# Attention: query units 6 to 8 projected whole in three steps, unit 9 in token halves

## The reference

```
proj = h @ w_in + b_in                        # (512, 1024) @ (1024, 1280)
q, k, v = split(proj, [1024, 1152])           # 16 query heads of 64, 2 key/value heads
q = q * 64 ** -0.5; k, v: previous and own block of 128 tokens
s = where(band, q @ k.T, -inf)                # band: the 128 latest keys
mx = max(max(s), sink)
p = exp(s - mx) / (sum(exp(s - mx)) + exp(sink - mx))
out = (p @ v) @ w_out + b_out
```

## Time and profile before

| | us |
|---|---|
| median of 3 runs | 1103.65 (1103.55 to 1104.68) |
| the profiled execution, its own time | 1103.78 |
| its span, first to last instruction | 1102.0 |
| TensorE busy | 1089.2 (99%) |
| VectorE busy | 532.7 (48%) |
| ScalarE busy | 430.8 (39%) |
| GpSimd busy | 51.5 (5%) |

### The profile page before, as it was taken

One profiled execution on the slowest core, in us unless ns is written; L12 is line 12 of the kernel. 1 busy time (PEld: TensorE's weight loads), 2 busy tenths in 40 slices (PEclk: granted clock), 3 DMA queues, 4 the chain that ended last, 5 costly groups with the idle time before them and its releaser, 6 DMA issues.

```text
span 1102.0 us, 14768 instructions
## 1 busy us (share of the span) xinstructions
PE 1089.2 (99%) x5562; PEld 911.0 (83%) x5562; DVE 532.7 (48%) x797; ACT 430.8 (39%) x750; POOL 51.5 (5%) x52
## 2 busy tenths in 40 slices
PE   9999998999999999999999999999999999999997
PEld 7888886898888888888889987789888888888886
DVE  7544567653434343333366586664444434523344
ACT  6511455543332323322255276754232323422242
POOL 1000210000000000000002023300000000000000
PEclk9999999999999999999999999999999999999999
DMA  8342327123233332122272632022323232303231
GB/s 267 112 116 80 112 95 212 38 78 114 84 107 92 98 99 92 39 95 95 95 191 59 162 87 77 1 67 87 114 77 114 76 114 78 112 26 101 99 136 77
DMA packets 141764, 109.51 MB, mean 99 GB/s; under 512 B 22480, under 2 KB 127088, under 8 KB 141728
## 3 DMA queue, kind: packets, MB, share of 16 engines
q1 hardware_dynamic: 140720, 105.84, 32.4%
q0 software_dynamic: 864, 2.92, 0.9%
q10 hardware_dynamic: 144, 0.26, 0.1%
HBM read 106.87 MB, written 2.13 MB: 99 GB/s over the span
## 4 chain that ended last, share of the span: by engine, by line
PE 92%; DVE 4%; ACT 3%; issue 0%; POOL 0%; DVEq 0%; ACTq 0%; POOLq 0%
PE ps L1461 17%; PE ps L1462 17%; PE ps L1463 17%; PE ps L1713 7%; PE ps L1711 7%; PE ps L1712 7%; PE ps L1656 3%; PE ps L1657 2%; PE ps L1658 2%; PE ps L1545 1%; PE ps L1547 1%; PE ps L1546 1%; PE ps L1801 1%; PE ps L1830 1%; PE ps L1812 1%; ACT w_hi L556 1%
## 5 line engine op out<-in xcount | busy, mean ns | idle before, releaser
L1461 PE MATMUL ps<-act_hi,w_hi 128*128 128x512 f32 (+1 forms) x1016 | 368.0, 362 | 0.1
L1463 PE MATMUL ps<-act_hi,w_lo 128*128 128x512 f32 (+1 forms) x1016 | 366.4, 361 | 0.0
L1462 PE MATMUL ps<-act_lo,w_hi 128*128 128x512 f32 (+1 forms) x1016 | 366.4, 361 | 0.0
L1461 PEld LDWEIGHTS ps<-act_hi,w_hi 128*128 128x128 f32 x1016 | 191.8, 189 | 30.8 <-DVE w_lo L916 0.9
L1463 PEld LDWEIGHTS ps<-act_hi,w_lo 128*128 128x128 f32 x1016 | 191.8, 189 | 29.3
L1462 PEld LDWEIGHTS ps<-act_lo,w_hi 128*128 128x128 f32 x1016 | 191.8, 189 | 28.7
L1711 PE MATMUL ps<-w_hi 128*128 128x512 f32 x288 | 112.0, 389 | 0.0
L1712 PE MATMUL ps<-w_lo,w_hi 128*128 128x512 f32 x288 | 112.0, 389 | 0.0
L1713 PE MATMUL ps<-w_hi,w_lo 128*128 128x512 f32 x288 | 112.0, 389 | 0.0
L749 ACT ACTIVATE arena<-ps,vecs 128x512 f32<-128x512 f32 x44 | 34.3, 780 | 188.6 <-PE ps L1463 188.6
L1242 DVE SCALAR_TENSOR_TENSOR arena<-ps,vecs,arena 128x511 f32<-128x511 f32 x44 | 33.0, 749 | 144.4 <-ACT arena L749 144.4
(11 more groups left out here) (210 smaller groups left out, 1220.1 us busy)
## 6 DMA issues: line engine op xcount, KB each, us to landing
raw<-in_f_w_up SPq DMA_DIRECT2D x88, 512.0 KB, 4.6
raw<-in_f_w_down SPq DMA_DIRECT2D x44, 512.0 KB, 3.3
raw<-in_m_w_in SPq DMA_DIRECT2D x23, 512.0 KB, 4.8
raw<-in_m_w_out SPq DMA_DIRECT2D x8, 512.0 KB, 3.4
raw<-in_a_w_in SPq DMA_DIRECT2D x16, 256.0 KB, 4.4
raw<-in_a_w_out SPq DMA_DIRECT2D x16, 256.0 KB, 4.8
h<-in_x SPq DMA_DIRECT2D x4, 512.0 KB, 7.4
h<-in_x_turned SPq DMA_DIRECT2D x3, 512.0 KB, 8.0
```

What stands on the lines that cost most here:

```text
L1461: nc.tensor.matmul(dst, uh[:, k], zh, start=(k == 0), stop=False)
L1462: nc.tensor.matmul(dst, uh[:, k], zl, start=False, stop=False)
L1463: ins = nc.tensor.matmul(dst, ul[:, k], zh, start=False, stop=(k == KT - 1))
```

## The change

Units 6, 7 and 8 are projected over all 512 tokens at once: unit 6 after scores(0), unit 7 in step 0, unit 8 in step 1. Unit 9 is projected in halves, at the head of steps 2 and 3, ahead of scores(s + 1). In step 2 turn_probs(2) now comes ahead of scores(3). VectorE adds the biases of units 6, 7 and 8 whole. That of unit 6 stands between the splits of units 8 and 9; those of 7 and 8 stand where the second halves stood in steps 0 and 1; the halves of unit 9 follow inverse(2) and inverse(3), ahead of masked_max. The counts that scores, the reuse of bank 5 and the first output part wait for are changed to match.

```diff
@@ add_a_bias (VectorE)
-                if n >= 6 and part == 0:
-                    dve.wait_ge(qb_mm, n - 5)
+                if n == A_UNITS - 1 and part == 0:
+                    dve.wait_ge(qb_mm, 1)
@@ VectorE, ahead of the steps
             masked_max(0)
-            for n in range(6, A_UNITS):
-                if n < 8:
-                    split_lo(G_AIN + n + 2)
-                add_a_bias(n, 0, 0, S // 2)
+            split_lo(G_AIN + 8)
+            add_a_bias(6)
+            split_lo(G_AIN + 9)
             dve.wait_ge(va_mm, 1)
@@ VectorE, step s
+                if s in (2, 3):
+                    add_a_bias(A_UNITS - 1, s - 2, (s - 2) * S // 2, (s - 1) * S // 2)
                 if s + 1 < AT_STEPS:
                     masked_max(s + 1)
                 if s >= 3 and s % 2 == 1:
                     mixed_lo((s - 3) // 2)
                 for k in OUT_SPLITS.get(s, []):
                     split_lo(G_AOUT + k)
-                if s < 4:
-                    add_a_bias(6 + s, 1, S // 2, S)
+                if s < 2:
+                    add_a_bias(7 + s)
@@ scores (TensorE)
-                pe.wait_ge(pj_used, QK_UNITS + (5 if s < 2 else A_UNITS if s < 6 else A_UNITS + 4))
+                pe.wait_ge(pj_used, QK_UNITS + (5 if s < 2 else 8 if s == 2 else A_UNITS + (s >= 2 * ASTEPS)))
@@ out (TensorE)
-                        pe.wait_ge(pj_used, QK_UNITS + A_UNITS + 4)
+                        pe.wait_ge(pj_used, QK_UNITS + A_UNITS + 1)
@@ TensorE
+            def query(n, lo=0, hi=S):
+
+                pe.wait_ge(w_lo_done, counted(G_AIN + n))
+                ins = project(SLOT[G_AIN + n], a_bank(n), lo, hi)
+                if hi == S:
+                    ins.then_inc(w_used, 1)
+                else:
+                    ins.then_inc(qb_mm, 1)
+
             scores(0)
-            for n in range(6, A_UNITS):
-                pe.wait_ge(w_lo_done, counted(G_AIN + n))
-                if n == 9:
-                    pe.wait_ge(pj_used, QK_UNITS + 7)
-                project(SLOT[G_AIN + n], a_bank(n), 0, S // 2).then_inc(qb_mm, 1)
+            query(6)
             turn_values()
...
             for s in range(AT_STEPS):
                 last = s + 1 == AT_STEPS
+                if s in (2, 3):
+                    pe.wait_ge(pj_used, QK_UNITS + (7 if s == 2 else A_UNITS))
+                    query(A_UNITS - 1, (s - 2) * S // 2, (s - 1) * S // 2)
+                if s == 2:
+                    turn_probs(s)
                 if not last:
                     scores(s + 1)
...
-                if s < 4:
-                    pe.wait_ge(pj_used, QK_UNITS + A_UNITS + s // 3)
-                    project(SLOT[G_AIN + 6 + s], a_bank(6 + s), S // 2, S).then_inc(w_used, 1)
-                turn_probs(s)
+                if s < 2:
+                    query(7 + s)
+                if s != 2:
+                    turn_probs(s)
```

## The result

The changed kernel takes 1108.69 us (median of 5 runs, 1107.62 to 1110.37) against 1104.61 for the kernel before; the ratio is 1.0041, 95% interval 1.0028 to 1.0054. It is slower, as forecast, but by 4.1 us at the median and not by 3.3, and 1108.69 lies above the range (1104.5 to 1108.3).

The account below looks back on a forecast made before the run. TensorE, busy 99% of the span, was taken to bound the kernel, so any wait there lengthens it. Terms -0.82 + 2.65 + 0.20 + 1.30 made +3.3 us, predicting 1107.0 us, range 1104.5 to 1108.3.

Parts of the forecast that it names:

- The clock falls: Rival: after the new idle stretch TensorE gets the lower clock for a unit, 5.5 us dearer, 1112.5 us; chance 0.04.
- Projection: TensorE's projection of units 6 to 9: fewer matmul starts take it from 23.52 to 22.70 us, a gain of 0.82.
- scores(2): TensorE idles 2.65 us (2.3 to 3.4) for unit 7's bias, queued on VectorE behind output weight 1's late load and split.
- Step 2: Ahead of scores(3), TensorE idles 0.20 us (0 to 0.4) for the bias of unit 9's first half.
- Steps 3 and 4: Softmax chain loses cover: idle 0.6 us ahead of scores(5), 0.7 ahead of step 4's transposes; together 1.3 (0.6 to 1.8).
- Step 3's own transposes: Block 0's softmax chain, 4.82 us plus 0.15, just covered by TensorE's 5.05 us of work; cost taken as 0.

Follow-up runs that it names:

- changed_again: The changed kernel, unaltered, measured once more on the same chip as the other runs: median 1107.88 us, ratio 1.0038 to the kernel before.
- half1_cut: Changed kernel with unit 9's second half cut in two, 12 matmuls ahead of scores(4), 12 behind mix(0), its bias moved: 1108.96 us, ratio 1.0039 to before.
- filled_transposes: Changed kernel with twenty unused 128x128 transposes in TensorE's idle stretch ahead of scores(2): median 1107.68 us, ratio 1.0032 to the kernel before.
- split9_first: Changed kernel with VectorE's split_lo of unit 9 put ahead of the bias of unit 6: median 1108.31 us, ratio 1.0039 to the kernel before.

## Why the prediction was wrong

The direction, the chain of waits and the sum of their terms were right; the step that failed is the rival "The clock falls". It had no term in the sum and no place in the range, and it came in the very execution that is the median: 1108.69 less its 1.57 us is 1107.12, and the forecast for the profiled execution was 1107.1. Term by term, from the timeline above:

- Projection: forecast -0.82. Queries 6 and 7 at 5.58 and 5.59 us, query 8 at 5.60 (in changed_again, without the fall) and two halves at 2.95 and 3.05 make 22.77 for 22.70: -0.75. The trace, with its 12 ns per start, was the right guide, and the 0.18 us estimated from the 2.5 ns of the Trainium skill ("TensorE: Matmul & The Clock Gate", section on 56 ns against 53.3 ns) would have been wrong.
- scores(2): forecast 2.65 (2.3 to 3.4). Measured 635.92 - 632.82 - 0.53 = 2.57, and in the same way 2.66 in changed_again and 3.17 in half1_cut. One small piece was read too short: a whole unit's bias begins 0.20 us after the block (626.26 behind 626.06), not 0.11.
- Step 2: forecast 0.20. The profile's wait is 0.23; by the starts it is 647.88 - 647.04 - 0.53 = 0.31, and the transposes of step 1 took 0.35 where I gave them 0.53: 0.13 together.
- Steps 3 and 4: forecast 0.6 + 0.7. Measured 654.79 - 653.65 - 0.53 = 0.61, and 659.38 - 655.86 - 2.90 = 0.62.
- Step 3's own transposes: forecast just covered; no wait shows there.
- The clock: "TensorE might be granted the lower clock for a unit", chance 0.04, price 5.5 us. The lower clock was granted for some 3.3 us and not for the whole unit, which costs 1.57 us, and it came in about five of the ten executions of this kernel (counted by time and mean clock). In the profiled one it makes +3.2 into +4.76, and it puts the median of the first set above the range. The size of this surplus is in part luck: the second set, with one such execution of five, has its median of 1107.88 inside the range.

Why I gave it 0.04: 1.7 us idle between 165 and 170 us at a clock of 1.00 was read as evidence that idle time does not matter. It was shorter than the wait that I forecast, and one execution. The trace of before has a second such case, which I had not read:

```profile
177.40 0.47 PE L1656 MATMUL ps<-w_hi,act_hi 128*128 128x512 f32 x1 [1.74 <-DVE w_lo L916]
```

All eleven profiled executions have both, 1.70 to 1.75 us each, at a granted clock of 1.00 from 165 to 185 us. So for 1.7 us the evidence is better than I knew, and for 2.2 to 3.1 us it does not hold: there two traces of four show the fall. The Trainium skill's rule ("TensorE: Matmul & The Clock Gate", "HAM oscillation") that gaps between bursts bring the clock down stood beside it, though the waits in that section's own case are longer than these. The changed kernel's windows agree with it (0.50 behind 2.51 us of idle time), changed_again's do not (1.00 behind 2.59). Had both been weighed, the case belonged inside the range with a chance near a half. That the same gap ends in a fall in one execution and not in another is shown; what decides it is open.

A second term was missing: the start. The first four matmuls of 512 columns, in the kernel before and in changed_again:

```profile
5.69 1.19 PE L1489 MATMUL ps<-act_hi,w_hi 128*128 128x512 f32 x4
```

```profile
5.71 2.01 PE L1490 MATMUL ps<-act_hi,w_hi 128*128 128x512 f32 x4
```

From their start to that of the next four it is 1.03 us in the one and 1.84 in the other, at a granted clock of 1.00 in both profiles. The rest of the kernel is later by it: scores(0) starts at 619.81, 619.84 and 620.58 in before, the changed kernel and changed_again. The profiled execution of before, from which I added up, was one without that delay. The delay is seen in kernels with and without the gap and is no effect of the change, but it widens what a range has to hold by up to 1 us. With it the profiled times add up: 1103.78, plus the change of the stretch, plus the lateness of scores(0), gives the time of each of the ten other profiled executions to 0.15 us (changed_again 1107.84 for 1107.83, the changed kernel 1108.57 for 1108.69). So the edits changed nothing outside the stretch.

The start and the fall go together in the few traces there are. Of the four with TensorE idle for over 2 us, the fall is in the two where scores(0) came early (619.84, 619.94), and not in the two where it came late (620.58, 620.80). An early start with the fall ends at 1108.7, a late one without it at 1107.8; the 1107.1 of the forecast needs an early start without the fall, and none of the ten executions is under 1107.62. filled_transposes, with an early start (620.01) and the gap filled, took 1107.53. Four traces can't show that the start decides on the fall, and nothing here tests it.

## What to carry to other kernels

A block moved on a saturated engine is cover for a chain elsewhere: before merging blocks to save starts (here some 10 ns each, 0.75 us in all), list for each step which chain the block was hiding, and the loop time that consecutive steps share on the other engines (here about 3.6 us a step). An addition that a saturated engine waits for must not stand behind an instruction that waits for a load; moving one line on VectorE was worth about 2.4 us of the 4 at the median. And where a change is expected to leave TensorE idle for longer than any stretch whose clock the trace shows, the chance of a fall belongs in the range, with its price (here 1.6 us).

## What the runs showed of the hardware

- The granted clock of TensorE was 0.50 for 3.3 us or more, beginning 1.5 us after work had resumed, behind an idle stretch of 2.51 us; the same, over 3.2 us, behind 3.10 us in half1_cut. Behind 2.59 us (changed_again) and 2.19 us (split9_first) it stayed at 1.00, and behind the two stretches of 1.7 us near 168 and 177 us it did so in all eleven profiled executions. One such fall cost 1.57 us.
- The first four matmuls of 512 columns took 1.03 us in one execution and 1.84 in another, both at a granted clock of 1.00 in the profile, and all that follows was later by it.
- Two pairs of 256 KB loads, from the second pair's last issue to the cast that uses it: 6.3 us when it was issued right behind the first pair (split9_first), 4.1 when issued 3.2 us behind it (the changed kernel). Issuing it 2.6 us earlier brought the cast 0.3 us forward. In the kernel before it took 5.0, also behind another pair.
